# Rotations, the memory's norm and the last convolution steps placed between the query tiles; squares added on GpSimd

## The chip, the cores and the metric

The kernel runs on one core of one Trainium2 chip. The metric is the device time of one execution in microseconds. Before the change it is 2010.14 us, the median of 3 runs (2008.37 to 2010.9).

A core has five engines that run their own instruction streams and meet at semaphores: TensorE (PE; its weight loads are listed apart as PEld), VectorE (DVE), ScalarE (ACT), GpSimd (POOL) and SyncE (SP, which here issues the large DMAs). SBUF is the on-chip memory. PSUM is the memory into which TensorE accumulates; the kernel uses it as two tiles, `acc` and `mis`, of four banks each.

## The reference

One layer of an encoder, for 256 prompt tokens and 32 sample tokens (288 columns in all), in float32. Only the start of the layer matters for this change:

```python
xn = rmsnorm(h, norm_mix_g)
proj = xn @ w_in                     # 2048 -> 1024 + 1024 (GLU), 1024 (queries), 256 (keys), 256 (values)
q = partial_rope(proj[queries], pos)
k = partial_rope(proj[keys], pos)
glu = a[..., :D_CONV] * sigmoid(a[..., D_CONV:])
y = depthwise_conv(glu, 31 taps)     # per channel, 1024 channels
y = silu(layernorm(y + dw_b, ln_g, ln_b))
attn = sliding_window_attention(q, k, v, sinks)   # 16 query heads, 4 key heads
h = h + concat(y, attn) @ w_out
# memory, 256 tokens of width 2048:
mn = rmsnorm(mem, norm_mem_g);  mk = mn @ w_ck;  mv = mn @ w_cv
h = h + cross_attention(rmsnorm(h), mk, mv)
h = h + peer_ffn(rmsnorm(h))         # expert retrieval, the largest part of the time
```

`partial_rope` multiplies with a cosine and adds a rotated copy multiplied with a sine. `rmsnorm` needs the sum of the squares over the 2048 channels, a square root and a reciprocal.

## The kernel before, in words

Channels lie on the 128 partitions and tokens along the free axis. A weight matrix streams through four raw buffers of 1 MB each. The stages around the change are these, in the order of TensorE's stream:

- GLU: 16 slots (16 weight tiles). VectorE begins the convolution of channel tiles 0, 1 and 2 in it.
- VKQ: 12 output tiles of the projection, n = 0 to 11: values (0, 1), keys (2, 3), queries (4 to 11). Each is 16 float32 matmuls of 128x288 (L1618; the profile counts two passes for each) into bank n % 4 of `acc`. VectorE takes each out of PSUM with one multiplication by the norm (`vkq`, L1018 or L1021) and counts it in `acc_free`. Behind it VectorE does 13 or 14 steps of the convolution (`conv`): a step is one tap of one channel tile, 128x318, a SCALAR_TENSOR_TENSOR with two operands in SBUF (L978). A channel tile has two first steps (L974, L976), 29 further ones, and a last step that adds the two accumulators into `y` (L964, L965). Five channel tiles, 160 steps, are spread over the 12 tiles.
- Behind VKQ, TensorE transposes the values (L1626), does rotations 0 and 1 (`turn`, L1639, L1641, L1642: a matmul with a fixed matrix into a bank of `mis`), adds the 16 tiles of the memory's squares up over the partitions (L1649) and does rotations 2 to 4. VectorE ends each rotation (`rope`, L1046, L1047, L1050). `ROPE = (0, 2, 3, 4, 5, 1, 6, 7, 8, 9)` is their order: 0 and 1 are key tiles, 2 to 9 are query tiles, and `ROPE_EARLY = 5` come ahead of the attention.
- Attention: 20 units, k = 0 to 19, with scores (L1663), softmax, transposes (L1675) and values (L1687) in a pipeline, filled up with the remaining rotations and with the memory's projection (`mem_part`, L1712). ScalarE takes the root of the memory's norm at k = 0 (`norm_root`), VectorE its reciprocal at k = 1 (`norm_recip`, L934 to L943).

The order of the work on each engine is written out by hand, as program order, and tables name the step k or the tile n at which a piece stands. Between the engines only semaphores hold the order: `rot_done` and `rope_done` for the rotations, `mem_sq` for ScalarE's squares of the memory (L589, four pieces of 128x1024), `mem_stat` for their sum, `rstd_done` for a finished reciprocal.

GpSimd adds the finished channel tiles of `y` up into `sqsum` (L1983, L1990), one addition of 128x288 when `conv_dve` counts the tile. Its first two stand right behind the stores of L1977 and L1978.

Of the kernel before, what the change touches and what calls it, by code (L numbers as in the profile page):

```python
# [25 lines left out]
ALU = mybir.AluOpType  # L26
# [40 lines left out]
CONV_HI_K = {14: (0, 2), 16: (2, 4), 17: (4, 6), 18: (6, 8)}  # L67
ROPE = (0, 2, 3, 4, 5, 1, 6, 7, 8, 9)
ROPE_EARLY = 5
RSTD = (1, 0, 0, 1, 0)  # L70
XROW_IT, HST_IT, TURN_S = 29, 30, 1
XROW_EVAC, HST_EVAC = 4 * XROW_IT + TURN_S + 1, 4 * HST_IT + TURN_S + 1
# [108 lines left out]
def build(nc, dr):  # L181
    swa = swa_units()
    ctx = ExitStack()
    with ctx:
# [155 lines left out]
        mem_sq, mem_ready, mem_stat = sem("mem_sq"), sem("mem_ready"), sem("mem_stat")  # L340
# [194 lines left out]
        def _(act):  # L535
# [59 lines left out]
            for n, (bank, ln, tiles) in enumerate(((0, P, (0, 2)), (1, P, (2, 3)), (2, CHUNK, (3, 4)), (3, NS, (4, 5)))):  # L595
                act.wait_ge(vt_done, 1 + n)
                nt = tiles[1] - tiles[0]
                act.activation(vtok[0:ln, tiles[0]:tiles[1], :],
                               mis[0:ln, bank, 0:256 * nt].rearrange("p (t c) -> p t c", t=nt), ACT.Copy).then_inc(vt_out, 1)

            def attention(A, hooks):
                S, units, n = A["sems"], A["units"], len(A["units"])
# [54 lines left out]
            def mem_root():  # L657
                norm_root(1, acc[:, 1], mem_stat, 1, MEM)

            def out_hi(n):  # L660
                hi_next(OUT0, 0, n - AHEAD)

            attention(SWA, {MEM_K0: mem_root, LN_K0 + 2: ln_squares, LN_K0 + 5: ln_rootf, **{k: lambda t=t: conv_silu(*t) for k, t in SILU_K.items()},
                            **{k: lambda t=t: conv_hi(*t) for k, t in CONV_HI_K.items()}, 20: lambda: out_hi(0), 21: lambda: out_hi(1)})
            for h in range(2):
                act.wait_ge(vt_done, 5 + h)
# [244 lines left out]
        def _(dve):  # L911
# [101 lines left out]
            def vkq(n):  # L1013

                s = n % 4
                slot_ready(VKQ0, 0, n)
                if n < 4:
                    dve.tensor_tensor(kvT[:, s, :], acc[:, s, 0:N], rstd[:, 1, :], ALU.mult).then_inc(acc_free, 1)  # L1018
                else:
                    for dst, src, r in q_parts(n - 4, acc[:, s, 0:N], rstd[:, 1, :]):  # L1020
                        ins = dve.tensor_tensor(dst, src, r, ALU.mult)  # L1021
                    ins.then_inc(acc_free, 1)
                steps = 32 * (CT - CONV_VKQ)
                for m in range(steps * n // 12, steps * (n + 1) // 12):
                    conv(CONV_VKQ + m // 32, False, m % 32, m % 32 + 1)

            def q_parts(t, *others):

                yield [qch[:, :, ds(t, 1), :].rearrange("p c a q -> p (c a) q")] + [
                    o[:, 0:NP_].rearrange("p (c q) -> p c q", q=CHUNK) for o in others]  # L1030
                yield [one(qsm[:, ds(t, 1), :])] + [o[:, NP_:N] for o in others]

            for n in range(12):
                vkq(n)

            def rope(n):

# [12 lines left out]
                    ins = dve.tensor_tensor(x, x, tmp, ALU.add)  # L1050
                ins.then_inc(rope_done, 1)

            for n in range(ROPE_EARLY):
                rope(n)

            def attention(A, hooks):
                S, units, n = A["sems"], A["units"], len(A["units"])
# [503 lines left out]
        def _(pe):  # L1561
# [50 lines left out]
            for n in range(12):  # L1612
                pe.wait_ge(raw_in[n % 4], 16 * (VKQ0 // 4 + n // 4 + 1))
                pe.wait_ge(acc_free, VKQ0 + n + 1)
                for j in range(DT):
                    if n == 0 and j % 4 == 0:
                        pe.wait_ge(xg_ready, j + 4)
                    ins = pe.matmul(acc[:, n % 4, 0:N], raw[:, n % 4, j, :], xg[:, j, :], start=(j == 0), stop=(j == DT - 1))  # L1618
                ins.then_inc(slot_used, 1)

            pe.wait_ge(rstd_done, 1)
            pe.wait_ge(acc_free, VKQ0 + 4 + 12)
            for n, (bank, starts, ln) in enumerate(((0, (0, P), P), (1, (CHUNK,), P), (2, (P + CHUNK,), CHUNK), (3, (NP_,), NS))):
                for a, k0 in enumerate(starts):
                    for j in range(2):
                        ins = pe.transpose(mis[0:ln, bank, 256 * a + P * j:256 * a + P * j + P], kvT[:, j, k0:k0 + ln], ident)  # L1626
                ins.then_inc(vt_done, 1)
# [17 lines left out]
            for n in range(2):  # L1645
                turn(n)
            pe.wait_ge(mem_sq, 4)
            for m in range(DT):
                ins = pe.matmul(acc[:, 1, 0:MEM], ones, memsq[:, m, :], start=(m == 0), stop=(m == DT - 1))  # L1649
            ins.then_inc(mem_stat, 1)  # L1650
            for n in range(2, ROPE_EARLY):
                turn(n)

            def attention(A, hooks, fill):
                S, units, n = A["sems"], A["units"], len(A["units"])
                for k in range(n + 3):
                    if k in hooks:
                        hooks[k]()
                    if k < n:
                        if k >= 2:  # L1660
                            pe.wait_ge(S["prob"], k - 1)
                        for out, q, keys in A["scores"](k, units[k]):
                            ins = pe.matmul(out, q, keys, start=True, stop=True)  # L1663
                        ins.then_inc(S["score"], 1)
                    for f in fill.get(k, ()):
                        f()
                    if 0 <= k - 2 < n:
                        un, r = units[k - 2], (k - 2) % 3
                        R = un["rows"]
                        pe.wait_ge(S["norm"], k - 1)  # L1670
                        if k >= 3:
                            pe.wait_ge(S["turnout"], k - 2)
                        for m, (a, ln, _) in enumerate(un["pieces"]):
                            for j in range(un["subs"]):
                                ins = pe.transpose(mis[0:ln, 2, 256 * m + P * j:256 * m + P * j + R],  # L1675
                                                   prob[0:R, r, 256 * j + a:256 * j + a + ln], ident[0:R, 0:R])
                        ins.then_inc(S["turned"], 1)
                    if 0 <= k - 3 < n:
                        un = units[k - 3]
                        pe.wait_ge(S["turnout"], k - 2)  # L1680
                        if k >= 4:
                            pe.wait_ge(S["vallo"], k - 3)
                        np_ = len(un["pieces"])
                        for j in range(un["subs"]):
                            for m in range(np_):
                                out, vals, pt = A["value"](un, j, m)
                                ins = pe.matmul(out, vals, pt, start=(m == 0), stop=(m == np_ - 1))  # L1687
                        ins.then_inc(S["value"], 1)

            def ln_sum():  # L1690
                pe.wait_ge(rstd_done, 2)
# [9 lines left out]
            pe.wait_ge(rope_done, ROPE_EARLY)  # L1701
            pe.wait_ge(vt_out, 4)
            pe.wait_ge(cache_in, 32)

            def mem_part(m, part):
                if part == 0:
# [243 lines left out]
        def _(pool):  # L1950
# [25 lines left out]
            pool.wait_ge(hist_in, 16)  # L1976
            pool.dma_start(dr["nconv_p"], glu[:, :, NP_:NP_ + HIST]).then_inc(early_out, 16)  # L1977
            pool.dma_start(dr["nconv_s"], glu[:, :, XW - HIST:XW]).then_inc(early_out, 16)  # L1978
            for t in range(1, CT - 1):
                pool.wait_ge(conv_dve, t + 1)  # L1980
                if t > 1:
# [256 lines left out]
```

## Time and profile before

| | us |
|---|---|
| median of 3 runs | 2010.14 |
| the profiled execution, its time | 2011.87 |
| the profiled execution, its span | 2010.0 |
| TensorE busy | 1969.0 (98%) |
| VectorE busy | 1526.5 (76%) |
| ScalarE busy | 863.6 (43%) |
| GpSimd busy | 709.3 (35%) |
| VKQ on TensorE, 384 passes | 93.28 |

The trace covers the span. A busy time is a sum of durations, so it tells little of a place: the places are read from rows in order of time. In such a row the first number is the start, the second the duration of the whole row, and `x13` means 13 instructions in it. A row of several pipelined instructions is as long as from the first start to the last end. The bracket behind it gives the time in which the engine sat idle ahead of it and what ended that. The granted clock is TensorE's, 1.00 for 2.4 GHz and 0.50 for 1.2 GHz.

### The profile page before, as it was taken

The page shows a single profiled execution, that of the slowest core. Times are in us where ns is not written, and L with a number is a line of the kernel's source. Part 1 is how long each engine was busy: PE and PEld are TensorE (multiplying, and loading weights), DVE is VectorE, ACT ScalarE, POOL GpSimd, SP SyncE. Part 2 cuts the span into 40 slices and gives each one's busy share as a digit, 9 for nine tenths or more (in the row PEclk, how much of TensorE's full clock was granted, in tenths as well). Part 3 has the DMA queues.
Part 4 walks back from the last instruction along what each step waited for, and adds up shares of the span by engine and source line. Part 5 has one row for each costly group of instructions (what it writes and reads, how often), then busy time and mean ns, then how long its engine had stood idle before and what let it go on. Part 6 is the DMA issues. An engine that isn't in the chain of part 4 may idle for free.

```text
span 2010.0 us, 29296 instructions
## 1 busy us (share of the span) xinstructions
PE 1969.0 (98%) x11128; PEld 1753.3 (87%) x11128; DVE 1526.5 (76%) x2291; ACT 863.6 (43%) x873; POOL 709.3 (35%) x488
## 2 busy tenths in 40 slices
PE   6999998999999999999999999999999999999998
PEld 6987776999999999999999999988888888888886
DVE  5988755455788898898889998577677767777786
ACT  4340136334544555445454555533343333344343
POOL 2010110220336687888868783010100101213310
PEclk9999998899999999999999999999999999999999
DMA  5464294444444778878887897889989899998984
GB/s 211 167 193 142 86 392 168 145 165 139 145 143 146 249 251 293 293 274 281 279 300 270 305 339 283 319 311 361 339 328 340 324 348 345 353 367 342 375 313 147
DMA packets 101226, 531.27 MB, mean 264 GB/s; under 512 B 19376, under 2 KB 21568, under 8 KB 45792
## 3 DMA queue, kind: packets, MB, share of 16 engines
q1 hardware_dynamic: 71552, 408.93, 56.8%
q0 software_dynamic: 24304, 106.45, 14.6%
q10 hardware_dynamic: 5296, 14.98, 2.0%
q8 instruction: 38, 0.62, 0.1%
q14 instruction: 36, 0.29, 0.0%
HBM read 491.34 MB, written 38.14 MB: 263 GB/s over the span
## 4 chain that ended last, share of the span: by engine, by line
PE 89%; DVE 5%; DMA 2%; ACT 2%; issue 1%; POOL 0%; DVEq 0%; SPq 0%; ACTq 0%; POOLq 0%
PE acc L1592 18%; PE mis L1939 17%; PE acc L1939 17%; PE acc L1593 9%; PE acc L1569 5%; PE acc L1571 5%; PE acc L1570 5%; PE acc L1618 5%; PE acc L1712 3%; DVE wl L917 1%; DMA raw<-in_u 1%; PE mis L1687 1%; ACT wh L540 1%; PE mis L1663 1%; DVE xhl L925 0%
## 5 line engine op out<-in xcount | busy, mean ns | idle before, releaser
L917 DVE TENSOR_TENSOR wl<-raw,wh 128x2048 fp32r<-128x2048 f32 x310 | 711.1, 2295 | 283.4 <-ACT wh L540 270.7
L540 ACT ACTIVATE wh<-raw 128x2048 fp32r<-128x2048 f32 x310 | 593.2, 1915 | 564.3 <-DMA raw<-in_v 409.3
L1592 PE MATMUL acc<-xhl,wh 128*128 128x448 f32 x2048 | 643.5, 375 | 1.4 <-DVE wl L917 1.2
L1593 PE MATMUL acc<-xhl,wl 128*128 128x224 f32 x2048 | 540.5, 264 | 0.0
L1592 PEld LDWEIGHTS acc<-xhl,wh 128*128 128x128 f32 x2048 | 384.2, 188 | 32.5 <-DVE wl L917 2.9
L1593 PEld LDWEIGHTS acc<-xhl,wl 128*128 128x128 f32 x2048 | 390.8, 191 | 0.0
L2094 POOL DMA_INDIRECT G<-gsum,cell x224 | 353.6, 1579 | 82.6 <-issue 69.8
L1569 PE MATMUL acc<-xhl,wh 128*128 128x288 f32 x768 | 230.4, 300 | 15.2 <-DVE wl L953 14.3
L1570 PE MATMUL acc<-xhl,wh 128*128 128x288 f32 x768 | 227.3, 296 | 0.0
L1571 PE MATMUL acc<-xhl,wl 128*128 128x288 f32 x768 | 226.9, 295 | 0.0
L1569 PEld LDWEIGHTS acc<-xhl,wh 128*128 128x128 f32 x768 | 145.4, 189 | 18.2 <-DVE wl L953 14.3
L2050 POOL DMA_INDIRECT ring<-in_ur,eidx x32 | 40.2, 1256 | 331.8 <-DVE hs L1397 323.3
L2050 POOL DMA_INDIRECT ring<-in_vr,eidx x32 | 78.5, 2452 | 215.4 <-DVE xrow L1485 179.6
L1570 PEld LDWEIGHTS acc<-xhl,wh 128*128 128x128 f32 x768 | 146.5, 191 | 0.1
L1571 PEld LDWEIGHTS acc<-xhl,wl 128*128 128x128 f32 x768 | 146.2, 190 | 0.0
L1939 PE MATMUL mis<-wh,ah 128*128 128x512 f32 x508 | 135.9, 389 | 0.0
L1939 PE MATMUL mis<-wh,al 128*128 128x512 f32 x508 | 135.8, 389 | 0.0
L1939 PE MATMUL mis<-wl,ah 128*128 128x512 f32 x508 | 135.8, 389 | 0.0
L1939 PE MATMUL acc<-wh,ah 128*128 128x512 f32 x508 | 135.8, 389 | 0.0
L1939 PE MATMUL acc<-wl,ah 128*128 128x512 f32 x508 | 135.8, 389 | 0.0
L1939 PE MATMUL acc<-wh,al 128*128 128x512 f32 x508 | 135.8, 389 | 0.0
L978 DVE SCALAR_TENSOR_TENSOR cacc<-glu,par,cacc 128x318 f32<-128x318 f32 x232 | 113.6, 561 | 0.5 <-DVE gsb L990 0.5
(323 smaller groups left out, 2585.3 us busy)
## 6 DMA issues: line engine op xcount, KB each, us to landing
raw<-in_u SPq DMA_DIRECT2D x128, 1024.0 KB
raw<-in_v SPq DMA_DIRECT2D x128, 1024.0 KB
raw<-in_w_mix SPq DMA_DIRECT2D x28, 1024.0 KB
G<-zero SPq DMA_DIRECT2D x16, 1024.0 KB, 14.0
raw<-in_w_out SPq DMA_DIRECT2D x16, 1024.0 KB
raw<-in_w_pq SPq DMA_DIRECT2D x16, 1024.0 KB
gin<-G SPq DMA_DIRECT2D x32, 512.0 KB
h<-hbg ACTq DMA_DIRECT2D x32, 448.0 KB
```

The source lines that it names most:

```text
L540: act.activation(wh[:, n % 4], raw[:, n % 4], ACT.Copy).then_inc(hi_done, 1)
L917: dve.tensor_tensor(wl[:, n % 4], raw[:, n % 4], wh[:, n % 4].bitcast(F32), ALU.subtract).then_inc(lo_done, 1)
L978: own.done(dve.scalar_tensor_tensor(cacc[:, a, :], x, w, cacc[:, a, :], ALU.mult, ALU.add))
L1569: pe.matmul(out, wh[:, wr, b, :], mh(j), start=(j == 0), stop=False)
L1570: pe.matmul(out, wh[:, wr, b, :], ml(j), start=False, stop=False)
L1571: ins = pe.matmul(out, wl[:, wr, b, :], mh(j), start=False, stop=(j == n - 1))
L1592: pe.matmul(acc[:, s, 0:2 * NU], wh[:, s, j, :], xu[:, j, 0:2 * NU], start=(j == 0), stop=False)
L1593: ins = pe.matmul(acc[:, s, 0:NU], wl[:, s, j, :], xuh[:, j, :], start=False, stop=(j == DT - 1))
L1618: ins = pe.matmul(acc[:, n % 4, 0:N], raw[:, n % 4, j, :], xg[:, j, :], start=(j == 0), stop=(j == DT - 1))
L1939: ins = pe.matmul(banks[t][c], ap[:, r, j, tok], w[:, s % 4, 4 * c:4 * c + 4, :].rearrange("p a n -> p (a n)"), start=False, stop=False)
L2050: pool.indirect_dma_start(ring[:, g % 2, :], None, dr["ur" if g < PICKS else "vr"], bass.IndirectOffsetOnAxis(ap=eidx[:, k:k + 1], axis=0) ...
L2094: pool.indirect_dma_start(cells_of, to, gsum[:, t, h, r:r + 1], None).then_inc(scattered[t], 16)
```

## The change

Four things change. All are in the stretch from the first VKQ tile to the first scores.

1. Rotations 0 to 4 no longer follow VKQ. TensorE does them behind tiles 4, 6, 7, 8 and 9 (`VKQ_TURN`), VectorE ends them behind its steps of tiles 5, 7, 8, 9 and 10 (`VKQ_ROPE`). `turn(n)` still waits for `rope_done >= n - 1`.
2. VectorE's convolution steps are no longer spread evenly but by `VKQ_CONV`, with 16 steps behind most of the first tiles and 4 behind the last.
3. GpSimd adds the four pieces of the memory's squares into one, so TensorE sums 4 tiles over the partitions in place of 16, and does it behind tile 8. ScalarE's root follows at once, and VectorE's reciprocal stands behind tile 10. GpSimd's three additions of 128x1024 stand ahead of all its additions of `y`.
4. The value transposes go to other banks of `mis`, stand behind VKQ as before, and now wait for the memory's reciprocal and for the fifth rotation.

```diff
+VKQ_TURN = {4: 0, 6: 1, 7: 2, 8: 3, 9: 4}
+VKQ_ROPE = {5: 0, 7: 1, 8: 2, 9: 3, 10: 4}
+VKQ_CONV = (16, 16, 16, 16, 16, 12, 16, 12, 12, 12, 12, 4)
+MEM_STAT, MEM_RECIP = 8, 10
...
@@ scalar
+            norm_root(1, mis[:, 3], mem_stat, 1, MEM)
...
-            attention(SWA, {MEM_K0: mem_root, ...
+            attention(SWA, {...
@@ vector, vkq(n)
-                steps = 32 * (CT - CONV_VKQ)
-                for m in range(steps * n // 12, steps * (n + 1) // 12):
+                for m in range(sum(VKQ_CONV[:n]), sum(VKQ_CONV[:n + 1])):
                     conv(CONV_VKQ + m // 32, False, m % 32, m % 32 + 1)
+                if n in VKQ_ROPE:
+                    rope(VKQ_ROPE[n])
+                if n == MEM_RECIP:
+                    norm_recip(1, mis[:, 3], MEM)
...
-            for n in range(ROPE_EARLY):
-                rope(n)
@@ vector, early(k)
-                if k == MEM_K0 + 1:
-                    norm_recip(1, acc[:, 1], MEM)
@@ tensor, turn(n)
-                if n < 2:
-                    pe.wait_ge(vt_out, 1 + n)
-                elif n < ROPE_EARLY:
-                    pe.wait_ge(rope_done, n - 1)
+                if n < ROPE_EARLY:
+                    pe.wait_ge(acc_free, VKQ0 + 4 + 2 + j + 1)
+                    if n >= 2:
+                        pe.wait_ge(rope_done, n - 1)
@@ tensor, VKQ
                 ins.then_inc(slot_used, 1)
+                if n in VKQ_TURN:
+                    turn(VKQ_TURN[n])
+                if n == MEM_STAT:
+                    pe.wait_ge(mem_added, 1)
+                    for m in range(4):
+                        ins = pe.matmul(mis[:, 3, 0:MEM], ones, memsq[:, m, :], start=(m == 0), stop=(m == 3))
+                    ins.then_inc(mem_stat, 1)
+
+            pe.wait_ge(rstd_done, 2)
+            pe.wait_ge(rope_done, ROPE_EARLY)
...
@@ gpsimd
+            for n in range(1, 4):
+                pool.wait_ge(mem_sq, n + 1)
+                if n > 1:
+                    own.wait(0)
+                ins = pool.tensor_tensor(memsq[:, 0:4, :], memsq[:, 0:4, :], memsq[:, 4 * n:4 * n + 4, :], ALU.add)
...
             for t in range(1, CT - 1):
                 pool.wait_ge(conv_dve, t + 1)
```

On TensorE, before, from the last VKQ tile (its 16 matmuls are the first two rows) to the first scores (L1663):

```order
L1618 MATMUL acc<-xg,raw 128x288 [waits acc_free,raw_in3]
L1618 MATMUL acc<-xg,raw 128x288 x15
L1626 MATMUL mis<-cst,kvT 128x128 [waits acc_free,rstd_done]
...
L1639 MATMUL mis<-kvT,cst 128x288 [waits vt_out]
L1641 MATMUL mis<-qch,cst 128x256 [waits vt_out]
L1642 MATMUL mis<-qsm,cst 128x32
L1649 MATMUL acc<-memsq,cst 128x256 [waits mem_sq]
L1649 MATMUL acc<-memsq,cst 128x256 x15
L1641 MATMUL mis<-qch,cst 128x256 [waits rope_done]
```

On TensorE, after the change, from tile 8 to tile 9 and then from tile 11 to the first scores (now L1668):

```order
L1635 MATMUL acc<-xg,raw 128x288 [waits acc_free,raw_in0]
L1635 MATMUL acc<-xg,raw 128x288 x15
L1625 MATMUL mis<-qch,cst 128x256 [waits rope_done,acc_free]
L1626 MATMUL mis<-qsm,cst 128x32
L1642 MATMUL mis<-memsq,cst 128x256 [waits mem_added]
L1642 MATMUL mis<-memsq,cst 128x256 x3
...
L1635 MATMUL acc<-xg,raw 128x288 [waits acc_free,raw_in3]
L1635 MATMUL acc<-xg,raw 128x288 x15
L1651 MATMUL mis<-cst,kvT 128x128 [waits rope_done,rstd_done]
...
L1668 MATMUL mis<-kvT,qch 128x64 [waits acc_free]
```

The fourth rotation (`turn(3)`, L1625) now stands between tiles 8 and 9 with its wait for `rope_done`, and everything behind it on TensorE waits with it.

On VectorE, after the change, from tile 7's multiplication to tile 8's (before, 13 steps of L978 stood there alone):

```order
L1023 TENSOR_TENSOR qch<-acc,rstd 128x4x64 [waits slot_used]
L1023 TENSOR_TENSOR qsm<-acc,rstd 128x32
L980 SCALAR_TENSOR_TENSOR cacc<-glu,par,cacc 128x318 [waits dve_own] x12
L1048 TENSOR_TENSOR sqt<-mis,cst 128x256 [waits rope_done,rot_done]
L1049 TENSOR_TENSOR qch<-qch,cst 128x4x64
L1048 TENSOR_TENSOR sqt<-mis,cst 128x32
L1049 TENSOR_TENSOR qsm<-qsm,cst 128x32
L1052 TENSOR_TENSOR qch<-qch,sqt 128x4x64 [waits dve_own]
L1052 TENSOR_TENSOR qsm<-qsm,sqt 128x32
L1023 TENSOR_TENSOR qch<-acc,rstd 128x4x64 [waits slot_used]
```

The six instructions L1048 to L1052 are `rope(1)`, the one for which `turn(3)` waits.

On GpSimd, after the change, from the two stores to the additions of `y`:

```order
L1978 DMA out_nconv_s<-glu 1024x1x30
L1983 TENSOR_TENSOR memsq<-memsq 128x1024 [waits mem_sq]
L1983 TENSOR_TENSOR memsq<-memsq 128x1024 [waits pool_own,mem_sq] x2
L1992 TENSOR_TENSOR sqsum<-y 128x288 [waits conv_dve]
L1992 TENSOR_TENSOR sqsum<-sqsum,y 128x288 [waits pool_own,conv_dve] x5
L1994 DMA ckT<-in_ckT 128x256 [waits slot_used]
```

The first three additions are new; the six of `y` follow them.

## Rows read from the trace of the kernel before

**Rows 1.** Waits of VectorE, 125 to 260 us: line, releaser, total, times, longest.

```profile
DVE qch L1021 <- PE acc L1618: 7.6, 8, 1.3
```

**Rows 2.** TensorE in order of time, from VKQ to the first scores.

```profile
127.43 93.28 PE L1618 MATMUL acc<-xg,raw 128*128 128x288 f32 x384
...
221.42 1.28 PE L1626 MATMUL mis<-cst,kvT 128*128 128x128 f32 x10 [0.70 <-DVE qsm L1021]
...
223.90 7.15 PE L1649 MATMUL acc<-memsq,cst 128*128 128x256 f32 x32
230.89 0.59 PE L1641 MATMUL mis<-qch,cst 128*128 128x256 f32 x2
...
236.48 1.11 PE L1663 MATMUL mis<-kvT,qch 64*128 64x64 f32 x4 [2.41 <-DVE qsm L1050]
```

**Rows 3.** VectorE in order of time, tiles 0, 5 and 7 of VKQ.

```profile
135.46 0.46 DVE L1018 TENSOR_TENSOR kvT<-acc,rstd 128x288 f32<-128x288 f32 x1 [2.45 <-PE acc L1618]
135.84 0.44 DVE L974 TENSOR_SCALAR cacc<-glu,par 128x318 f32<-128x318 f32 x1
...
136.49 5.15 DVE L978 SCALAR_TENSOR_TENSOR cacc<-glu,par,cacc 128x318 f32<-128x318 f32 x11
...
174.19 0.42 DVE L1021 TENSOR_TENSOR qch<-acc,rstd 128x256 f32<-128x256 f32 x1 [0.72 <-PE acc L1618]
...
174.63 6.53 DVE L978 SCALAR_TENSOR_TENSOR cacc<-glu,par,cacc 128x318 f32<-128x318 f32 x14
...
191.19 0.43 DVE L964 TENSOR_TENSOR y<-cacc 128x256 f32<-128x256 f32 x1
...
191.75 1.02 DVE L974 TENSOR_SCALAR cacc<-glu,par 128x318 f32<-128x318 f32 x1
...
192.99 3.76 DVE L978 SCALAR_TENSOR_TENSOR cacc<-glu,par,cacc 128x318 f32<-128x318 f32 x8
```

**Rows 4.** GpSimd and VectorE at the same time, three places.

```profile
123.13 1.17 DVE L978 SCALAR_TENSOR_TENSOR cacc<-glu,par,cacc 128x318 f32<-128x318 f32 x1
...
123.15 0.81 POOL L1973 TENSOR_TENSOR gsb<-gsb,rstd 128x288 f32<-128x288 f32 x1 [9.98 <-ACT gsb L578]
...
191.79 0.80 POOL L1983 TENSOR_TENSOR sqsum<-sqsum,y 128x288 f32<-128x288 f32 x1 [18.80 <-DVE y L965]
...
556.70 4.12 DVE L917 TENSOR_TENSOR wl<-raw,wh 128x2048 fp32r<-128x2048 f32 x1
```

**Rows 5.** All instructions of two lines: duration min/median/max ns, first and last start.

```profile
L917 DVE TENSOR_TENSOR wl<-raw,wh x310: 2273/2291/4119, 21.5 to 1986.3; 128x2048 fp32r<-128x2048 f32 x155
...
L2041 POOL TENSOR_TENSOR xn<-hT,rstd x4: 2371/3406/4452, 549.5 to 558.6; 128x1024 f32<-128x1024 f32 x4
```

**Rows 6.** ScalarE's last three squares of the memory.

```profile
142.32 1.06 ACT L589 ACTIVATE memsq<-memT 128x1024 f32<-128x1024 f32 x1 [1.75 <-DMA memT<-in_memT]
...
147.70 1.04 ACT L589 ACTIVATE memsq<-memT 128x1024 f32<-128x1024 f32 x1
```

**Rows 7.** VectorE: a query and a key rotation, and the memory's reciprocal, first and last.

```profile
231.66 0.42 DVE L1046 TENSOR_TENSOR sqt<-mis,cst 128x256 f32<-128x256 f32 x1 [0.54 <-PE mis L1642]
...
233.00 0.18 DVE L1050 TENSOR_TENSOR qsm<-qsm,sqt 128x32 f32<-128x32 f32 x1
...
238.94 0.46 DVE L1046 TENSOR_TENSOR sqt<-acc,cst 128x288 f32<-128x288 f32 x1 [2.52 <-PE acc L1639]
...
239.80 0.46 DVE L1050 TENSOR_TENSOR kvT<-kvT,sqt 128x288 f32<-128x288 f32 x1
...
247.11 1.75 DVE L934 RECIPROCAL rstd<-root 128x256 f32<-128x256 f32 x1
...
250.59 0.43 DVE L943 TENSOR_TENSOR rstd<-rstd,root 128x256 f32<-128x256 f32 x1
```

**Rows 8.** Granted clock: window, its length, PE busy, PEclk, DMA share, GB/s.

```profile
236.00:242.00 6.00, 5.52 (x14) 0.50 0.03 9
318.00:327.00 9.00, 9.00 (x27) 0.50 0.02 7
```

More of the change, by code:

```diff
@@ L339, in build @@
         xg_ready = sem("xg_ready")
-        mem_sq, mem_ready, mem_stat = sem("mem_sq"), sem("mem_ready"), sem("mem_stat")
+        mem_sq, mem_ready, mem_stat, mem_added = sem("mem_sq"), sem("mem_ready"), sem("mem_stat"), sem("mem_added")
         raw_in = [sem(f"raw_in{n}") for n in range(RAW)]
@@ L593, in _ @@
                 ins.then_inc(mem_ready, 1)
-            for n, (bank, ln, tiles) in enumerate(((0, P, (0, 2)), (1, P, (2, 3)), (2, CHUNK, (3, 4)), (3, NS, (4, 5)))):
-                act.wait_ge(vt_done, 1 + n)
+            norm_root(1, mis[:, 3], mem_stat, 1, MEM)
+            for n, (bank, at, ln, tiles) in enumerate(((2, 0, P, (0, 2)), (3, 0, P, (2, 3)), (3, 256, CHUNK, (3, 4)), (1, 0, NS, (4, 5)))):
+                act.wait_ge(vt_done, 3 if n == 1 else 1 + n)
                 nt = tiles[1] - tiles[0]
                 act.activation(vtok[0:ln, tiles[0]:tiles[1], :],
-                               mis[0:ln, bank, 0:256 * nt].rearrange("p (t c) -> p t c", t=nt), ACT.Copy).then_inc(vt_out, 1)
+                               mis[0:ln, bank, at:at + 256 * nt].rearrange("p (t c) -> p t c", t=nt), ACT.Copy).then_inc(vt_out, 1)
             def attention(A, hooks):
@@ L655, in conv_hi @@
                     act.activation(xh[:, t, :], y[:, t, :], ACT.Copy).then_inc(split_hi, 1)
-            def mem_root():
-                norm_root(1, acc[:, 1], mem_stat, 1, MEM)
             def out_hi(n):
                 hi_next(OUT0, 0, n - AHEAD)
-            attention(SWA, {MEM_K0: mem_root, LN_K0 + 2: ln_squares, LN_K0 + 5: ln_rootf, **{k: lambda t=t: conv_silu(*t) for k, t in SILU_K.items()},
+            attention(SWA, {LN_K0 + 2: ln_squares, LN_K0 + 5: ln_rootf, **{k: lambda t=t: conv_silu(*t) for k, t in SILU_K.items()},
                             **{k: lambda t=t: conv_hi(*t) for k, t in CONV_HI_K.items()}, 20: lambda: out_hi(0), 21: lambda: out_hi(1)})
@@ L1031, in q_parts @@
                 yield [one(qsm[:, ds(t, 1), :])] + [o[:, NP_:N] for o in others]
-            for n in range(12):
-                vkq(n)
             def rope(n):
@@ L1051, in rope @@
                 ins.then_inc(rope_done, 1)
-            for n in range(ROPE_EARLY):
-                rope(n)
+            for n in range(12):
+                vkq(n)
             def attention(A, hooks):
@@ L1611, in _ @@
                     slot(GLU0, i, s, xh, xl)
[L1612 to L1627, printed above, removed]
             def turn(n):
                 j = ROPE[n]
-                if n < 2:
-                    pe.wait_ge(vt_out, 1 + n)
-                elif n < ROPE_EARLY:
-                    pe.wait_ge(rope_done, n - 1)
+                if n < ROPE_EARLY:
+                    pe.wait_ge(acc_free, VKQ0 + 4 + 2 + j + 1)
+                    if n >= 2:
+                        pe.wait_ge(rope_done, n - 1)
                 else:
@@ L1643, in turn @@
                 ins.then_inc(rot_done, 1)
[L1645 to L1652, printed above, removed]
+            for n in range(12):
+                pe.wait_ge(raw_in[n % 4], 16 * (VKQ0 // 4 + n // 4 + 1))
+                pe.wait_ge(acc_free, VKQ0 + n + 1)
+                for j in range(DT):
+                    if n == 0 and j % 4 == 0:
+                        pe.wait_ge(xg_ready, j + 4)
+                    ins = pe.matmul(acc[:, n % 4, 0:N], raw[:, n % 4, j, :], xg[:, j, :], start=(j == 0), stop=(j == DT - 1))
+                ins.then_inc(slot_used, 1)
+                if n in VKQ_TURN:
[7 more added lines that the diff above has]
+            pe.wait_ge(rope_done, ROPE_EARLY)
+            for bank, at, starts, ln in ((2, 0, (0, P), P), (3, 0, (CHUNK,), P), (3, 256, (P + CHUNK,), CHUNK), (1, 0, (NP_,), NS)):
+                for a, k0 in enumerate(starts):
+                    for j in range(2):
+                        c = at + 256 * a + P * j
+                        ins = pe.transpose(mis[0:ln, bank, c:c + P], kvT[:, j, k0:k0 + ln], ident)
+                ins.then_inc(vt_done, 1)
+            pe.wait_ge(acc_free, VKQ0 + 4 + 12)
             def attention(A, hooks, fill):
@@ L1659, in attention @@
                     if k < n:
+                        if k == 1:
+                            pe.wait_ge(vt_out, 4)
                         if k >= 2:
                             pe.wait_ge(S["prob"], k - 1)
+                        if units[k]["kind"] == "sample":
+                            pe.wait_ge(cache_in, 32)
                         for out, q, keys in A["scores"](k, units[k]):
@@ L1690, in ln_sum @@
             def ln_sum():
-                pe.wait_ge(rstd_done, 2)
                 pe.wait_ge(ln_added, 1)
@@ L1699, in ln_varf @@
                 ins.then_inc(ln_var, 1)
-            pe.wait_ge(rope_done, ROPE_EARLY)
-            pe.wait_ge(vt_out, 4)
-            pe.wait_ge(cache_in, 32)
             def mem_part(m, part):
@@ L1978, in _ @@
             pool.dma_start(dr["nconv_s"], glu[:, :, XW - HIST:XW]).then_inc(early_out, 16)
+            for n in range(1, 4):
[3 more added lines that the diff above has]
+                ins = pool.tensor_tensor(memsq[:, 0:4, :], memsq[:, 0:4, :], memsq[:, 4 * n:4 * n + 4, :], ALU.add)
+                if n < 3:
+                    own.done(ins)
+                else:
+                    ins.then_inc(mem_added, 1)
             for t in range(1, CT - 1):
```

## The prediction

> **What bounds the kernel now.** I read the page first. TensorE is busy for 98% of the span, so what counts is what it does or waits for. Next came TensorE's waits: in the stretch of the change they are all for VectorE, mostly for its rotations. Then the timeline of TensorE, where a wait stands in the bracket at a row's end. VKQ runs without a gap from 127.43 for 93.28 us, 7.77 us a tile. From its end (220.72) to the first scores (236.48) lie 15.8 us: the value transposes 1.3, the sum of the memory's squares 7.15, five rotations at about 0.6, and gaps: 0.7 ahead of the transposes, 2.4 ahead of the first scores, and the rest, 1.2, between the rotations [rows 2]. These 15.8 us are what the change can win from. Last, the timelines of VectorE, ScalarE and GpSimd in VKQ, since the moved work goes there. VectorE does 13 or 14 convolution steps a tile and then waits for TensorE's next tile, 7.6 us in all for the eight query tiles [rows 1]. A tile has about 1 us of room on VectorE.
>
> **What TensorE does less.** The sum of squares goes from 16 tiles to 4. It is 7.15 us in 32 passes, 0.223 each, so 24 passes or 5.4 us go and 1.8 stay [rows 2]. Rotations and transposes stay, in other places. The gaps go as such. So far that is 5.4 + 0.7 + 2.4 + 1.2 = 9.7 us less, if nothing new is waited for. Two new waits are possible: `turn(3)` behind tile 8 waits for `rope(1)`, and the transposes behind tile 11 wait for the memory's reciprocal.
>
> **When VectorE is done with rope(1).** VectorE begins tile 0 at 135.46 [rows 3] and has, up to the end of `rope(1)` behind tile 7:
> - 8 multiplications out of PSUM: 0.38 for each of four (135.46 to 135.84) and about 0.44 for each of four query tiles: 3.3 us.
> - 120 convolution steps (5 x 16 + 12 + 16 + 12), which are 109 steps of L978 at 0.46 (5.15 us for 11, less the tail of the last): 50.3. Four pairs of first steps: 0.65 us for the first pair (135.84 to 136.49), 1.24 for the three others (191.75 to 192.99, with GpSimd's addition of `y` in it): 4.4. Three last steps at 0.56 (191.19 to 191.75): 1.7 [rows 3].
> - `rope(0)` 1.3 and `rope(1)` 1.5 (238.94 to 240.26, 231.66 to 233.18) [rows 7]: 2.8.
>
> That is 62.5 us without GpSimd's new additions, so VectorE would reach 198.2, some tenths later with small waits. TensorE is there at 127.43 + 9 x 7.77 + 3 x 0.6 = 199.2. It would just not wait. The plan closes with under 1 us of slack, which is why the next item decides.
>
> **What GpSimd's additions cost VectorE.** The trace shows that a VectorE instruction with two SBUF operands stands still while GpSimd runs a TENSOR_TENSOR. A convolution step that met one of 0.81 us took 1.17 us where its kind takes 0.54 (5.15 us less ten steps of 0.46), so 0.63 more. The first step at 191.75 took 1.02 beside an addition of 0.80, where the one at 135.84 took 0.44. At a larger size, an L917 took 4.12 us at 556.70 where the median is 2.29 [rows 3 to 5]. So GpSimd's length less about 0.2 us is lost. A GpSimd TENSOR_TENSOR of 128x1024 took at least 2.37 us [rows 5]. Three make 3 x 2.2 = 6.6 us. The bounds are 3 x 1.83 = 5.5 (the loss of that L917) and 3 x 2.37 = 7.1, and nothing at all if they do not meet such steps. They do meet them: they become ready at 143.4 and 148.7, the ends of ScalarE's squares [rows 6], with one between. VectorE is then in tile 1, which has 16 steps and no idle time. The first two additions of `y`, which ran at about 130 and 133 just ahead of an idle time, move behind them: 2 x 0.6 = 1.2 us more. VectorE's multiplications out of PSUM have one SBUF operand and I take them as unhindered.
>
> The Trainium skill (SBUF — State Buffer, section "SBUF: two separate sides") says that VectorE and GpSimd share one pair of ports under an exclusive lock, that a VectorE operation with two SBUF inputs needs it against a GpSimd operation that reads SBUF, and that the loser blocks fully, for the whole instruction. By that rule the three additions would cost 3 x 2.37 = 7.1 us, by the rows 6.6. It speaks against this change.
>
> So `rope(1)` ends at 198.2 + 0.2 + 6.6 + 1.2 = 206.2 and TensorE waits for it some 7 us, from 199.2. The `acc_free` waits do not bind: VectorE may be three tiles behind and is at most two. `turn(1)` and `turn(2)` need tile 4's multiplication at about 175 and `rope(0)` at about 190.4, and stand at 182.4 and 190.8.
>
> **From there to the first scores.** Behind `turn(3)` on TensorE: 0.6, the sum 1.8, tile 9 7.8, `turn(4)` 0.6, tile 10 7.8: 206.3 + 18.6 = 224.9. The clock comes on top. After two pauses of TensorE, the 2.4 us ahead of the first scores [rows 2] and one near 316 us, the granted clock was 0.50 for six and nine whole microseconds, nearly all with TensorE busy [rows 8]. A pause of 7 us should do the same. With 5.5 to 10 us of busy time at 1.2 GHz it costs 2.8 to 5; I take 3.3, nearer to the first. Tile 10 ends at 228.2.
>
> VectorE, which has caught up in tile 9, then does tile 10's multiplication 0.4, 12 steps 5.5, `rope(4)` 1.5 and the reciprocal 3.9 (247.11 to 251.02 [rows 7]), with 0.4 of handing over: 240.0. TensorE ends tile 11 at 236.0 and waits 4 us. Then transposes at a low clock, 1.9 in place of 1.3, and the first scores at 241.8. Before it was 236.48. That is +5.3; I say +5.1, since up to 0.3 of the handing over is counted twice.
>
> **The attention.** It is TensorE's own time from 236.48 on, with the clock low in its first 5.8 us [rows 8], which cost 2.9. The new pause of 4 us should bring the same again. VectorE loses the reciprocal there (3.9) and gets four steps (2.0), both beside TensorE's memory matmuls: nothing. ScalarE's root moves to its idle time. The copies of the values out of PSUM must be through before unit 1; they have the memory's matmuls of unit 0 as cover. GpSimd's stores wait for the sixth rotation as before. Behind this the kernel is TensorE's, so the shift goes through to the end.
>
> **Sum.** 2011.87 of the profiled execution, which is 2010.0 of span and 1.87 around it, becomes 2017.0. It lies 1.7 above the median of the runs. For the median: 2010.14 + 5.1 = 2015.2. Own range: 5.5 to 8.7 for VectorE's loss, 2.8 to 5 for the clock, 1 either way for the second pause: +1.5 to +9.
>
> **The rivals.** About 0.2%, 4 us, is what a measurement can tell from no change.
> - *VectorE's loss never reaches TensorE* (the additions cost VectorE little, or slip into its pauses). Then `turn(3)` does not wait: tile 9 from 199.2 + 0.6 + 1.8, tile 10 ends at 217.8, the reciprocal at 229.6, the scores come at 230.9 with the clock as before: -5.6, 2004.5. Faster. For it: the plan closes without the additions. Against it: the rows of GpSimd and VectorE side by side. It decides from a loss of under 1 us. Chance 0.17.
> - *The loss is there, the clock is not.* `turn(3)` waits 7 us, but the clock stays at 2.4 GHz, or falls within the pause and is back at its end. Then tile 10 ends at 224.9, the reciprocal at 236.7, the scores at 238.0: +1.5; if it stays up in the attention too, 2.9 less. Between -1.4 and +1.5, say 2010.9. Same. Against it: both pauses above 2 us were followed by the low level. Chance 0.18.
> - *The clock stays low for ten microseconds after each pause.* +1.7 for the first and +2.1 for the second: 2019. Slower. Chance 0.08.
>
> **How the numbers follow.** My forecast has 0.57; about three quarters of its range lies above +4, so it gives 0.42 to slower and 0.15 to same. With the rivals: slower 0.50, same 0.33, faster 0.17. The range reaches down to 2005, which takes in about half of the first rival, and up to 2020.
>
> **What would show it.** GpSimd's three additions of 128x1024 between 143 and 152, with VectorE's steps of 2.5 us beside them; VectorE behind by some 8 us in tiles 2 to 5; TensorE's wait for `rope(1)` ahead of the fourth rotation, 6 to 8 us, and one of about 4 us ahead of the transposes; the granted clock at 0.50 behind both. No wait at the fourth rotation would make the forecast wrong, and so would VectorE's steps of 0.54 us beside GpSimd's additions.

## The result, and the profile after

The changed kernel takes 2013.83 us (median of 13 runs, 2010.85 to 2017.01), the kernel before 2009.65 (13 runs, 2007.64 to 2012.48) beside it. The ratio is 1.0016 with a 95% interval of 1.0008 to 1.0023. So it is slower: by 4.2 us going by the two medians, by 3.2 going by the ratio. That is near the edge of what can be told from no change, but the interval lies above 1. The forecast was 2015.2, or +5.1. The profiled execution took 2017.01 us, its span is 2015.2.

First TensorE's waits from 100 to 420 us in the changed kernel (line, releaser, total, times, longest):

```profile
PE mis L1625 <- DVE qsm L1052: 5.6, 1, 5.6
PE mis L1680 <- ACT probT L618: 4.9, 3, 2.3
PE mis L1651 <- DVE rstd L945: 3.6, 1, 3.6
PE mis L1692 <- DVE xhl L1066: 2.3, 3, 1.1
```

The two waits for ScalarE (L1680) and for `xhl` (L1692) belong to the attention and are there before too. The two others are new: the one for `rope(1)` ahead of the fourth rotation, and the one for the memory's reciprocal ahead of the transposes. TensorE in order of time, after, beside [rows 2]:

```profile
206.32 1.19 PE L1625 MATMUL mis<-qch,cst 128*128 128x256 f32 x2 [5.58 <-DVE qsm L1052]
...
207.59 3.76 PE L1642 MATMUL mis<-memsq,cst 128*128 128x256 f32 x8
211.14 8.27 PE L1635 MATMUL acc<-xg,raw 128*128 128x288 f32 x32
219.25 0.59 PE L1625 MATMUL mis<-qch,cst 128*128 128x256 f32 x2
...
219.82 15.77 PE L1635 MATMUL acc<-xg,raw 128*128 128x288 f32 x64
...
239.22 2.40 PE L1651 MATMUL mis<-cst,kvT 128*128 128x128 f32 x10 [3.63 <-DVE rstd L945]
241.55 1.11 PE L1668 MATMUL mis<-kvT,qch 64*128 64x64 f32 x4
```

Read the durations as well as the brackets. The fourth rotation takes 1.19 us where its kind takes 0.59; the sum over four tiles takes 3.76 for 8 passes, 0.47 each where [rows 2] have 0.223; the ten transposes take 2.40 instead of 1.28. Each is at half the clock behind its wait. The four stretches with a low clock between 100 and 650 us (window, length, PE busy, PEclk, DMA share, GB/s), after:

```profile
205.00:212.00 7.00, 5.68 (x15) 0.51 0.01 2
239.00:246.00 7.00, 6.78 (x22) 0.51 0.21 85
324.00:328.00 4.00, 4.00 (x12) 0.57 0.02 6
351.00:363.00 12.00, 9.09 (x41) 0.57 0.43 147
```

The trace of before has three such stretches, none near 205. The one near 320 is longer there:

```profile
235.00:243.00 8.00, 6.52 (x18) 0.57 0.12 33
317.00:328.00 11.00, 10.39 (x31) 0.53 0.04 16
351.00:363.00 12.00, 9.37 (x41) 0.57 0.31 115
```

VectorE in order of time, after, tiles 1 and 4, then the multiplications behind tiles 9 and 10 and the reciprocal:

```profile
144.66 0.46 DVE L1020 TENSOR_TENSOR kvT<-acc,rstd 128x288 f32<-128x288 f32 x1
145.04 14.26 DVE L980 SCALAR_TENSOR_TENSOR cacc<-glu,par,cacc 128x318 f32<-128x318 f32 x15
...
167.94 6.98 DVE L980 SCALAR_TENSOR_TENSOR cacc<-glu,par,cacc 128x318 f32<-128x318 f32 x15
...
205.99 0.18 DVE L1052 TENSOR_TENSOR qsm<-qsm,sqt 128x32 f32<-128x32 f32 x1
...
219.45 0.43 DVE L1023 TENSOR_TENSOR qch<-acc,rstd 128x256 f32<-128x256 f32 x1 [5.37 <-PE acc L1635]
...
227.87 0.42 DVE L1023 TENSOR_TENSOR qch<-acc,rstd 128x256 f32<-128x256 f32 x1 [0.94 <-PE acc L1635]
...
235.26 1.75 DVE L936 RECIPROCAL rstd<-root 128x256 f32<-128x256 f32 x1
```

And GpSimd in the same stretch, after:

```profile
144.84 2.36 POOL L1983 TENSOR_TENSOR memsq<-memsq 128x1024 f32<-128x1024 f32 x1 [13.08 <-ACT memsq L593]
147.51 5.29 POOL L1983 TENSOR_TENSOR memsq<-memsq 128x1024 f32<-128x1024 f32 x2 [0.31 <-ACT memsq L593]
152.76 1.05 POOL L1992 TENSOR_TENSOR sqsum<-y 128x288 f32<-128x288 f32 x1
153.95 0.85 POOL L1992 TENSOR_TENSOR sqsum<-sqsum,y 128x288 f32<-128x288 f32 x1
```

Fifteen equal steps take 14.26 us beside GpSimd's five additions (three large, two of `y`), and 6.98 where GpSimd rests: 7.3 us lost. The first of them alone took 2.52 where its kind takes 0.54. The multiplication out of PSUM at 144.66 took its usual 0.46, but it began ahead of the first addition; a cleaner case stands below, with the additions done twice.

TensorE's busy time in the span went from 1969.0 to 1965.6 us, and the kernel is still slower.

### The profile page after: what moved, and what is told of

It reads as the page before. It is cut to its first block, busy times and chain, and to the rows that moved or that the text cites. A ratio compares the mean times of both kernels' runs of the same rounds, so it can differ in the third digit from the quotient of the medians.

```text
span 2015.2 us, 29258 instructions
## 1 busy us (share of the span) xinstructions
PE 1965.6 (98%) x11104; PEld 1749.6 (87%) x11104; DVE 1530.6 (76%) x2291; ACT 862.8 (43%) x873; POOL 719.4 (36%) x491
## 4 chain that ended last, share of the span: by engine, by line
PE 83%; DVE 10%; issue 3%; DMA 2%; ACT 2%; POOL 0%; DVEq 0%; SPq 0%; ACTq 0%; POOLq 0%
PE mis L1939 17%; PE acc L1939 17%; PE acc L1592 16%; PE acc L1593 8%; PE acc L1569 5%; PE acc L1571 5%; PE acc L1570 5%; DVE cacc L980 3%; PE acc L1712 3%; DVE wl L919 2%; PE acc L1635 2%; DMA raw<-in_u 1%; PE mis L1692 1%; ACT wh L544 1%; PE mis L1668 1%
## 5 line engine op out<-in xcount | busy, mean ns | idle before, releaser
L1592 PE MATMUL acc<-xhl,wh 128*128 128x448 f32 x2048 | 644.2, 375 | 3.8 <-DVE wl L919 3.8
L1592 PEld LDWEIGHTS acc<-xhl,wh 128*128 128x128 f32 x2048 | 384.0, 188 | 35.9 <-DVE wl L919 6.2
L2103 POOL DMA_INDIRECT G<-gsum,cell x224 | 347.9, 1553 | 81.6 <-issue 70.1
L980 DVE SCALAR_TENSOR_TENSOR cacc<-glu,par,cacc 128x318 f32<-128x318 f32 x232 | 119.7, 586 | 0.5 <-DVE gsb L992 0.5
```

Of the source, the lines that this page charges most:

```text
L980: own.done(dve.scalar_tensor_tensor(cacc[:, a, :], x, w, cacc[:, a, :], ALU.mult, ALU.add))
L1592: pe.matmul(acc[:, s, 0:2 * NU], wh[:, s, j, :], xu[:, j, 0:2 * NU], start=(j == 0), stop=False)
L2103: pool.indirect_dma_start(cells_of, to, gsum[:, t, h, r:r + 1], None).then_inc(scattered[t], 16)
```

## What was tried

The theory: the change gives back on TensorE about what it takes away in work, since VectorE comes late in two places, and what makes it slower is the time at 1.2 GHz behind the new waits. No run separates the clock from the waits, so this second half rests on comparing stretches and mean clocks. The rival that took most runs to weigh: the extra time has nothing to do with these waits and comes from a later stage. No kernel here leaves out part of the computation. Each was compared with the kernel before on its own chip.

**Both kernels again.** The same two texts, for how much a trace and a median move by themselves.

> The changed kernel once more, for a second trace of it. Theory A (VectorE is held up by GpSimd's additions, TensorE waits for rope(1) and for the memory's reciprocal, and the clock falls behind both): +4 us against the kernel before, and the distance from the first VKQ matmul to the first scores again about 3.5 us longer than before (112.6 against 109.1). Theory B (the extra time arises elsewhere: up to the first expert matmul the two profiled executions differ by only 0.7 us, and 3.3 come in the stage behind it, where TensorE waited 10.1 against 4.2 us for VectorE's weight splits): the first expert matmul again within 1 us of before, the rest of the 4 us in the expert stage.

> The kernel before against itself. Both theories: ratio 1.000 with an interval of about 0.001. Its trace tells how much the stages vary from execution to execution: theory A expects TensorE's waits for VectorE's weight splits in the expert stage to vary by several us between traces of one kernel; theory B expects them to stay near 4 us, as in the first trace.

Measured: 2013.95 (11 runs), ratio 1.002 (1.0011 to 1.0029), and 2010.26 (11 runs), ratio 1.0002 (0.9992 to 1.0013). The change is slower again by about the same amount (the ratio makes it 4.0 us). Its first scores come 112.0 us behind the first VKQ matmul, where the first trace has 112.6 and the kernel before 109.1. TensorE's waits in the repeated trace of the changed kernel, 100 to 420 us:

```profile
PE mis L1625 <- DVE qsm L1052: 5.5, 1, 5.5
...
PE mis L1651 <- DVE rstd L945: 3.6, 1, 3.6
```

They are the same within 0.1 us, so they belong to the kernel. This execution was the fastest of its 11, with 2008.55 us. In the expert stage TensorE waited 2.0 us for VectorE's weight splits here and 4.3 in the second trace of before, which by itself still fitted the rival's 4 us for that kernel; the third trace below did not.

**Without GpSimd's additions.** The rotations and the root stay between the tiles; the sum goes over all 16 tiles again.

```
-                    pe.wait_ge(mem_added, 1)
-                    for m in range(4):
-                        ... memsq[:, m, :], start=(m == 0), stop=(m == 3))
+                    pe.wait_ge(mem_sq, 4)
+                    for m in range(DT):
+                        ... memsq[:, m, :], start=(m == 0), stop=(m == DT - 1))
...
-            for n in range(1, 4):            # GpSimd: the three additions
-                ...
```

> The changed kernel, but GpSimd adds nothing of the memory's squares; TensorE sums all 16 tiles behind tile 8, 5.4 us more work. Theory A: VectorE is not held up, the wait for rope(1) ahead of the fourth rotation (5.6 us) is under 1 us, the clock does not fall there, the wait for the reciprocal stays at 3.5 to 4; the first scores come 109.5 us after the first VKQ matmul, 3 us less than in the changed kernel; time 3 us below the changed kernel, within 1.5 us of the kernel before. Rival (VectorE is late because of its 16 steps a tile, not because of GpSimd): the wait for rope(1) stays near 5 us, and the time is 5 us above the changed kernel.

Measured: 2010.25 (12 runs), ratio 0.9998 (0.9989 to 1.0008), 3.7 us less than the changed kernel. TensorE in order of time:

```profile
199.53 0.59 PE L1625 MATMUL mis<-qch,cst 128*128 128x256 f32 x2
...
200.10 7.15 PE L1642 MATMUL mis<-memsq,cst 128*128 128x256 f32 x32
...
234.83 2.40 PE L1651 MATMUL mis<-cst,kvT 128*128 128x128 f32 x10 [3.63 <-DVE rstd L945]
```

The fourth rotation has no bracket: VectorE is in time, as the prediction's count without the additions had it. `rope(1)` ends at 198.79, 0.7 us ahead of TensorE; the prediction had 0.8. The first scores come 109.3 us behind the first VKQ matmul (109.5 expected). VectorE's 15 steps of tile 1 are back at 6.99 us:

```profile
144.00 6.99 DVE L980 SCALAR_TENSOR_TENSOR cacc<-glu,par,cacc 128x318 f32<-128x318 f32 x15
```

TensorE does 5.4 us more work than in the changed kernel, and the kernel is faster. At these places in the program the additions cost more than they save. The wait for the reciprocal stays at 3.63.

**The additions twice.** Each addition is done once more into a tile that is free at that time; the rest is untouched.

```
+                own.done(pool.tensor_tensor(mkvT[:, 0:4, :], memsq[:, 0:4, :], memsq[:, 4 * n:4 * n + 4, :], ALU.add))
+                own.wait(0)
                 ins = pool.tensor_tensor(memsq[:, 0:4, :], memsq[:, 0:4, :], memsq[:, 4 * n:4 * n + 4, :], ALU.add)
```

> The changed kernel with each of GpSimd's three additions of 128x1024 done twice (the first into a tile that is not used yet). Theory A: VectorE loses 2.2 us more for each, 6.6 in all; the wait for rope(1) grows from 5.6 to about 12 us; time 6 to 7 us above the changed kernel, 10 above before. Rival (GpSimd's additions find room beside VectorE): the wait stays at 5.6 us and the time as that of the changed kernel.

Measured: 2018.7 (6 runs), ratio 1.0043 (1.0031 to 1.0055), 4.8 us above the changed kernel; 6 to 7 were expected. TensorE waits 4.2 and 5.4 us for the two rotations, where one wait of about 12 was expected. VectorE's row of tile 1, and then TensorE's rotations:

```profile
144.75 20.20 DVE L980 SCALAR_TENSOR_TENSOR cacc<-glu,par,cacc 128x318 f32<-128x318 f32 x15
```

```profile
196.27 0.67 PE L1625 MATMUL mis<-qch,cst 128*128 128x256 f32 x2 [4.23 <-DVE kvT L1052]
...
211.97 1.19 PE L1625 MATMUL mis<-qch,cst 128*128 128x256 f32 x2 [5.36 <-DVE qsm L1052]
```

The same 15 steps: 6.99 without additions, 14.26 with three, 20.20 with six. The second three cost 5.9 us, 2.0 each. On TensorE this comes as one more wait, at the third rotation, and the first scores come 118.7 us behind the first VKQ matmul, where the changed kernel has 112.6 and 112.0.

This trace also has a multiplication out of PSUM that began while a large addition was running. It took its usual 0.46 us:

```profile
144.22 2.36 POOL L1983 TENSOR_TENSOR mkvT<-memsq 128x1024 f32<-128x1024 f32 x1 [12.74 <-ACT memsq L593]
```

```profile
144.38 0.46 DVE L1020 TENSOR_TENSOR kvT<-acc,rstd 128x288 f32<-128x288 f32 x1
```

**The reciprocal one tile earlier.**

```
-MEM_STAT, MEM_RECIP = 8, 10
+MEM_STAT, MEM_RECIP = 8, 9
```

> The changed kernel with the memory's reciprocal on VectorE behind tile 9 in place of tile 10 (VectorE sits idle there for 5.4 us). Theory A (both waits count, each with its fall of the clock): the wait of 3.6 us ahead of the value transposes goes down to about 0.3, the wait for rope(1) stays at 5.6, the clock no longer falls at the start of the attention; time 3.5 to 6.5 us below the changed kernel, 0 to 2 below before. Rival (the wait only moves: TensorE then waits for rope(4) or for the convolution's last steps): at most 1 us.

Measured: 2012.88 (11 runs), ratio 1.0014 (1.0004 to 1.0023), where the changed kernel had 1.0016 and 1.002: about 1 us less or nothing, which the noise does not tell apart, where 3.5 to 6.5 less were expected. It came out as the rival said, the wait only moved. TensorE's waits, 100 to 420 us:

```profile
PE mis L1625 <- DVE qsm L1052: 5.7, 1, 5.7
...
PE mis L1651 <- DVE qsm L1052: 2.8, 1, 2.8
```

The wait for the reciprocal is gone, and at the same transposes stands one for `rope(4)`, at 2.8 us. VectorE's free time lies ahead of tile 9's multiplication:

```profile
217.23 0.42 DVE L1023 TENSOR_TENSOR qch<-acc,rstd 128x256 f32<-128x256 f32 x1 [4.38 <-PE acc L1635]
```

What it has to do from there (the multiplication, 12 steps, a rotation, the reciprocal: 11.3 us) is longer than a tile of TensorE, so it passes its lateness on. One number moved is not enough.

**The steps spread evenly**, otherwise the changed kernel:

```
-VKQ_CONV = (16, 16, 16, 16, 16, 12, 16, 12, 12, 12, 12, 4)
+VKQ_CONV = (13, 13, 14, 13, 13, 14, 13, 13, 14, 13, 13, 14)
```

> The changed kernel with its convolution steps spread as before the change, 13 or 14 behind each tile. Up to tile 7 these are 106 steps in place of 120, 6.4 us less on VectorE. Theory A (TensorE's wait for rope(1) is VectorE's plan plus GpSimd's additions, whichever gives way): the wait of 5.6 us ahead of the fourth rotation goes to under 1 us and with it the fall of the clock there; the wait for the reciprocal grows from 3.6 to about 4.5, and 14 steps in place of 4 stand ahead of the sixth rotation, 4.6 us, which TensorE meets at unit 1. First scores about 105 us after the first VKQ matmul (112.3 in the changed kernel, 109.1 before); time 3 to 7 us below the changed kernel. Rival (14 steps behind tile 11 delay the attention as much as is won): same time as the changed kernel within 1.5 us.

Measured: 2007.65 (11 runs), ratio 0.999 (0.9981 to 0.9999), 5 to 6 us below the changed kernel by the ratios. TensorE's waits, 100 to 420 us:

```profile
PE mis L1651 <- DVE rstd L945: 4.1, 1, 4.1
...
PE mis L1625 <- DVE qsm L1052: 1.5, 1, 1.5
```

The additions are all there, yet the wait at the fourth rotation is 1.5 instead of 5.6 (under 1 was expected). Up to tile 7 VectorE has 14 steps less, 6.4 us, of which it idles away 1.5 ahead of tile 1's multiplication. The rest gives it room for most of the 7.3. The first scores come 106.3 us behind the first VKQ matmul (about 105 expected). The wait that was expected at the sixth rotation, behind the 14 steps of tile 11, is not there.

**Room made for VectorE.** The reciprocal behind tile 9, fewer steps in tiles 2 to 11, and 19 steps into the first rotations of the attention:

```
-VKQ_CONV = (16, 16, 16, 16, 16, 12, 16, 12, 12, 12, 12, 4)
-MEM_STAT, MEM_RECIP = 8, 10
+VKQ_CONV = (16, 16, 12, 12, 12, 12, 11, 12, 16, 5, 13, 4)
+MEM_STAT, MEM_RECIP = 8, 9
+LATE_CONV = (4, 4, 4, 4, 3)
...
+                if k < len(LATE_CONV):        # in early(k), behind its rotation
+                    at = sum(VKQ_CONV) + sum(LATE_CONV[:k])
+                    for m in range(at, at + LATE_CONV[k]):
+                        conv(CONV_VKQ + m // 32, False, m % 32, m % 32 + 1)
```

> The changed kernel with fewer convolution steps between the tiles, so that VectorE has room for what GpSimd's additions cost it: VKQ_CONV = 16 16 12 12 12 12 11 12 16 5 13 4, the reciprocal behind tile 9, and the 19 steps left over behind rotations 5 to 9 in units 0 to 4 of the attention. Theory A: no wait at the fourth rotation (under 1 us) and none at the transposes, no fall of the clock at either; the first scores 99.5 to 101 us after the first VKQ matmul (109.1 before, 112.3 in the changed kernel); time 8 to 12 us below before, 12 to 15 below the changed kernel. Rival (VectorE's late steps hold up the attention's first units): TensorE waits for VectorE in units 1 to 6, and half or more of the gain is lost.

Measured: 1999.68 (5 runs), ratio 0.994 (0.9927 to 0.9954). By the ratios it beats the kernel before by 12 us and the changed kernel by about 15. TensorE in order of time, and the clock of the whole stretch:

```profile
199.40 0.60 PE L1630 MATMUL mis<-qch,cst 128*128 128x256 f32 x2
...
226.84 1.28 PE L1656 MATMUL mis<-cst,kvT 128*128 128x128 f32 x10 [0.96 <-DVE qsm L1053]
228.05 0.66 PE L1673 MATMUL mis<-kvT,qch 64*128 64x64 f32 x4
```

```profile
185.00:300.00 115.00, 114.04 (x543) 1.00 0.71 258
```

No wait at the fourth rotation, one of 0.96 us at the transposes, and the full clock through both places: TensorE is busy for 114.04 of 115 us. The first scores come 100.3 us behind the first VKQ matmul; 109.1 before, 112.6 changed. The rival, that the 19 late steps hold up the attention, has nothing for it: the waits in the attention are those of the other kernels (4.8 us for ScalarE, 2.3 for `xhl`). The gain is that of three edits together; it was not divided among them.

**The same without the additions**, with the edit that took them out above:

> The same as the paced kernel, but GpSimd adds nothing of the memory's squares and TensorE sums all 16 tiles behind tile 8. It gives the worth of the additions where VectorE has room for them. Theory A: TensorE's 5.4 us more work is all there is, time 5 to 6 us above the paced kernel. Rival (what GpSimd's additions cost VectorE cancels what they save TensorE, paced or not): same time as the paced kernel within 1.5 us.

Measured: 2004.71 (7 runs), ratio 0.9969 (0.9958 to 0.998), 5.0 us above the one with additions. Once VectorE has room, the 24 passes that GpSimd saves TensorE are worth almost their own 5.4 us. Where it has none, they cost 3.7.

**The kernel before, a third trace.** A single execution.

> One look at the kernel before, for a third trace of it. Its runs have a mean granted clock of 0.992 to 0.996, those of the changed kernel 0.990 to 0.992 with one of 0.993. Theory A: an execution of the kernel before with a mean clock of 0.994 or more lacks one of the stretches at 1.2 GHz that the first two traces have (at 235, 317 and 351 us), and is some 3 us shorter up to the first expert matmul. Rival: the stretches are the same and the time differs in the expert stage.

Measured: 2013.57 us, span 2011.8. Its windows at a low clock:

```profile
236.00:241.00 5.00, 4.32 (x13) 0.66 0.00 0
318.00:326.00 8.00, 8.00 (x25) 0.57 0.00 1
349.00:357.00 8.00, 5.81 (x26) 0.57 0.42 160
```

They begin about where those of the first trace begin and are shorter. One was expected to be missing, and none is. The 3 us that were expected up to the experts are there. This trace decided the rival. From the first VKQ matmul to the first of the experts lie 522.6, 520.8 and 518.4 us in the three traces of before, and 521.8 and 520.7 in the two of the changed kernel: taken as they are, no clear difference. TensorE's busy time at 1.2 GHz up to there, added up over windows of one microsecond, is 24.3, 21.0 and 15.0 us before, 23.0 and 21.6 changed. At that clock work takes twice its time, so half of this busy time is what the clock costs. Take it off and 510.4, 510.3 and 510.9 are left before, 510.3 and 509.9 changed. The same working gives 509.5 without the additions, 516.0 with the additions twice, 506.6 evenly spread, 501.9 paced and 507.2 paced without additions. At an equal clock, then, the additions are worth about nothing where VectorE has no room (509.5 against 510.1). Most of the 3.7 us between these two kernels is the clock's: 17.4 us busy at 1.2 GHz without the additions, 22.3 in the mean of the changed kernel's two traces, which is 2.4 us more lost.

The rival's stage needs no part in it. What TensorE waits for VectorE there (L1592) was 4.2 and 4.3 us in the first two traces of before and 10.1 after, but 15.1 in this one. The rows after the change and in this trace:

```profile
DVE wl L919: 10.1, 16
DVE wl L917: 15.1, 17
```

In the repeated trace of the changed kernel it was 2.0. These waits change from execution to execution of one kernel.

## Why the prediction came out as it did

The direction and the chain of causes held. By its own steps:

- **GpSimd's additions cost VectorE, and in tile 1.** They ran from 144.8 to 152.8 in the 15 steps of tile 1. Predicted were 6.6 for them and 1.2 for the additions of `y` behind them, 7.8; measured 7.3, of which the run with the additions twice puts 2.0 on each of the large ones. The rule in the Trainium skill (SBUF — State Buffer, section "SBUF: two separate sides") would have three full lengths for the large ones, 2.36, 2.42 and 2.73, or 7.5 us; the loss is about 0.5 an addition less. It agrees in kind, and so does the multiplication out of PSUM that began inside an addition and was not held up.
- **The wait at the fourth rotation.** 5.6 us, predicted 7. VKQ begins 1.5 us later in this trace. Counted from there TensorE arrived as predicted (200.7, or 71.8 behind its start), and VectorE, done at 206.2, was 1.5 us quicker than its count. Of this 0.5 is the additions. Another 0.2 is a sum that does not come out (135.46 + 62.5 is 198.0, not 198.2), and 0.2 are small waits that were not there. The last 0.6 is spread over the small terms of the 62.5 us.
- **The clock behind it.** From 205 to 212 at 1.2 GHz with 5.68 us busy: 2.8 lost, predicted 3.3.
- **The reciprocal's wait.** 3.63 us, predicted 4. VectorE went from tile 10's multiplication to the end of the reciprocal in 11.3 us (227.87 to 239.17), as counted. The first scores came 112.6 us behind the first VKQ matmul, and 112.0 in the repeated trace, against 109.1: +3.5 and +2.9, predicted +5.3. The mis-sized terms are the 1.5 us of VectorE's count and 0.5 of the clock.
- **The old gaps and the work went** as counted: 5.4 for the sum and 4.3 of gaps, 9.7; the new waits are 5.6 + 3.6 = 9.2. At an equal clock the change is worth nothing (-0.4 by the distances above, which scatter by as much). What is left for the loss is the clock.
- **"As before" for the attention: the step that was weak.** The prediction read the clock of before from one execution, in which it was low for long: 27 us up to the experts, where the third trace has 17. In the 61 runs of before made beside these experiments the mean granted clock lay between 0.992 and 0.996. The 24 runs at 0.994 or above took 2008.6 us in the mean, the 37 below 2011.5. A pair of traces cannot show a difference of 3 us against that, medians can. The mean over these runs is 0.9936 before and, over the 24 runs of the changed kernel, 0.9917. The difference of 0.0019 is about 8 us more at half the clock (0.0019 x 2012 / 0.5). TensorE was busy for 0.79 to 0.89 of these stretches in the five traces, so 3.0 to 3.4 us are lost. That is an estimate from means, and it meets the 3.2 of the ratio. The run without additions has 0.993, the paced one 0.9946.
- **"The shift goes through to the end".** The third trace of before has a mean clock of 0.994, near the mean of the runs; the other two lie lower (0.991 by its low stretches, and 0.992). Against the third, the changed kernel is 3.4 and 2.3 us later at the first expert matmul, and was 3.5 and 2.9 later at the first scores: the shift goes through. Against the other two it seems lost. The prediction also missed that the low stretch near 320 us gets shorter. It lasted 10, 7 and 7 us in the traces of before, and 3 in both of the changed kernel. Why is not shown.
- **The rivals.** That VectorE's loss never reaches TensorE has two waits against it. "The loss is there, the clock is not" would give a kernel equal to the one before, as the distances at an equal clock show. Ten microseconds after each pause did not come in the changed kernel: the stretches around the two new waits were 7 us in both traces. In the evenly spread kernel the one around the wait of 4.1 us did last 10.

Open is what decides in one execution whether a low stretch lasts 3, 7 or 10 us, and why the low stretch behind the 2.4 us gap of the kernel before lasted 7 us in two traces and 3 in the third. That was not tried.

## What to carry over

Before work goes to GpSimd to spare TensorE, ask what VectorE does at that moment. Beside convolution steps with two operands in SBUF, a large addition, 2.4 to 2.7 us long, took 2.0 us from VectorE. It saves TensorE time only if VectorE has that room before TensorE next waits for it. When work is moved between the steps of the bound engine, pace the helper's list against each place where the bound engine now waits; here that list and 19 steps moved into the attention were worth some 15 us, while the change itself cost 3 to 4. And where a pause lowers the clock, compare mean clocks over many runs, since one trace shows one draw.

## What was unexpected of the hardware

- The stretches at 1.2 GHz start at about the same places in each trace of a kernel and last about 3, 7 or 10 us from one execution to the next. Up to the experts they add up to 27, 24 and 17 us in three traces of before.
- A pause of 0.96 us left the clock at full speed (the paced kernel, 1.00 from 185 to 300 us), and so did the wait of 1.5 us in the evenly spread one. The waits of 2.8 to 5.7 us in the changed stretch came with a stretch at half the clock in every trace here, and so did the 2.4 us gap before. The length of one pause does not say it all: near 350 us in the first trace of before the clock also fell, behind pauses of 1.57 and 1.04 us that came close together.
- Two traces of one kernel, 2015.2 and 2006.7 us long, agree within 0.1 us in both waits for VectorE in the changed stretch: their difference lies elsewhere.
